# Feed-forwards: the Strassen form from the third gate/up pair on, with the sums of activations made in the first two pairs

## The chip, the cores and the metric

One NeuronCore of one Trainium2 chip runs the whole program. The metric is device time in microseconds (us) of one execution, lower is better. TensorE (PE) multiplies matrices, VectorE (DVE) and ScalarE (ACT) do elementwise work, GpSimd (POOL) does a little, and SyncE (SP) issues nearly all transfers. Each engine runs its own instructions in program order and waits for the others on semaphores.

## The reference

One layer of a streaming encoder for 640 tokens (512 of a new stream, 8 x 16 of running ones) at width 1024, in f32:

```
x += 1/2 * g1 * SwiGLU_1(mod1(RMSNorm(x)))
x += g2 * W_out [ gMLP groups || SSD heads ] (W_in mod2(RMSNorm(x)))
x += 1/2 * g3 * SwiGLU_2(mod3(RMSNorm(x)))
def swiglu(h, w1, w2):
    g, u = jnp.split(h @ w1, 2, axis=-1)
    return (jax.nn.silu(g) * u) @ w2
```

`w1` is 1024 x 5632 and `w2` is 2816 x 1024. A final modulated RMSNorm and some state outputs follow. Only the two SwiGLU feed-forwards (the first and the third line) are touched here.

## The kernel before, in words

**Precision.** Every f32 matmul is made of three reduced-precision ones: weights and activations are each split into a high part (an ACT copy into type fp32r) and a low part (DVE: value minus high part), and PE adds high x high, high x low and low x high. A weight block is therefore prepared by one ACT instruction (`blk` on ACT, L1547) and one DVE instruction (`blk` on DVE, L2122), each 128x512, before PE may read its slot. There are 7 slots (`SLOTS`) in a ring, and two buffers `raw` for the transfers (one "job" each, `load_job`).

**Feed-forward.** The hidden width 2816 is 22 tiles of 128. For each tile there is a gate/up pair `p`: the gate columns and the up columns times the 1024 rows of `hn`. Pairs come in parts of 4, 4, 4, 4, 3 and 3 (`PARTS`), and after each part its down products (eight blocks, `BLK_DOWN`) are added to `xT`.

**Two forms of a pair.** `plain_pair` multiplies 4 weight blocks (gate and up, each over two halves of the rows): 4 blocks x 4 tiles of rows x 3 products x 2 halves of the tokens = 96 matmuls of 320 columns. `wino_pair` treats the pair as a 2x2 block product (gate/up by row halves, row halves by token halves) and uses the Strassen-Winograd form with 7 products instead of 8: 7 x 4 x 3 = 84 matmuls. It needs sums of weight blocks (`first_sums` and two in `blk`: four DVE additions, L2085, in the raw buffer, `s1w`, `s2w`) and four sums of activations, T1 to T4. Pairs 0 to `PLAIN - 1` are plain, the rest Strassen. Before, `PLAIN = 3`.

**The sums of activations** are made once per feed-forward, for kk = 0 to 3. `t_sums(kk)` on DVE (L2256 to L2261) makes four 128x320 sums; `t_high(kk)` on ACT (L1686, L1687) copies the high part of T2 (320 columns) and T3, T4 (640 columns) into `tT`; `t_low(kk)` on DVE (L2267, L2269) makes the low parts. Temporaries `tst`, `xadd`, `rT` take turns over kk. T1 is handled apart: `t1_high` on ACT (L1693) and `t1_low` on DVE (L2278) overwrite a quarter of `hn_hi`, `hn_lo`, and so come after the last plain product.

**Order of the queues before.** Block numbers run through the feed-forward; plain pairs 0, 1, 2 have blocks 0 to 3, 4 to 7, 8 to 11, and Strassen pair 3 has 12 to 18. While pair `p` with first block `b` is multiplied, ACT and DVE prepare blocks `b+7` to `b+10` (or `b+13` for Strassen).

- ACT, pair 0: SiLU of gate (L1707), `t_high(0)`, blocks 7, 8, `hid_high` (L1699), blocks 9, 10. Pair 1: `t_high(1)`, SiLU, `t_high(2)`, blocks 11, 12, `hid_high`, 13, 14. Pair 2: SiLU, `t_high(3)`, 15, 16, `t1_high`, `hid_high`, 17, 18.
- DVE, pair 0: `t_sums(0)`, gate x up into `hidp` (L2303), `t_low(0)`, 7, 8, `hid_low` (L2284), 9, 10. Pair 1: `t_sums(1)`, `t_low(1)`, `t_sums(2)`, `hidp`, `t_low(2)`, 11, 12, `hid_low`, 13, 14. Pair 2: `t_sums(3)`, `t_low(3)`, 15, 16, `hidp`, `t1_low`, `hid_low`, 17, 18.

DVE reaches `t_sums(0)` only after the norm and blocks 4 to 6.

**What the first Strassen pair waits for** (`wino_pair` on PE, L1067 for the matmuls): after its first product P (bank pC), for all SiLUs of the plain pairs and for `t_ready`, that is the last `t_low`; after the second product for the snapshot of P (`snap` 1, ACT, L1730), because the third product adds onto the same bank; before the fifth for `t1_low`. ACT comes to that snapshot only when its work for the last plain pair is through.

```
product(fi, b, x, b11, True)
if p == PLAIN:
    pe.wait_ge(silu_done, fi * N_PAIR + p)
    pe.wait_ge(t_ready, 6 * fi + KQ)
product(fi, b + 1, z_bank, t3, True)
if cols is not None and p == PLAIN:
    duo_cols(cols)
pe.wait_ge(snap, 4 * n + 1)
product(fi, b + 2, x, t2, False)
```

**Between the pairs** of the first feed-forward stand small products of the conditioning vectors ("duos": `duo_rows` L966 behind pairs 1, 2, 5, 7 and so on, `duo_row` on ACT, `duo_cols` L977 on PE, `duo_sum` on DVE, L2222). In the second one they stand behind pairs 3 and 7, and two at pair 0. A transfer into `raw` waits until the low parts of the job two before are made (SP, L601, L606).

Of the kernel before, what the change touches and what calls it, by code (L numbers as in the profile page):

```python
# [25 lines left out]
FF_TILES = D_FF // P  # L26
PARTS = (4, 4, 4, 4, 3, 3)
PART0 = (0, 4, 8, 12, 16, 19)
PLAIN = 3
KQ = KD // 2  # L30
WB = KQ * P
SLOTS = 7
# [52 lines left out]
def trunk_program(nc, x_prompt, x_sample, state_ssm, state_conv, c_prompt, c_sample, w_ada, b_ada, norm_g,  # L85
# [5 lines left out]
    def sb(name, shape, dt=F32, stack=None):  # L91
        return (stack or top).enter_context(nc.sbuf_tensor(name, shape, dt))
# [13 lines left out]
    slots = [sb(f"slot{i}", [P, 2 * WB], F32R, wbuf) for i in range(4)]  # L106
# [280 lines left out]
    def t34_f(kk):  # L387
        return (xadd, rT)[kk % 2]
# [35 lines left out]
    for part, kh in enumerate(PARTS):  # L424
        for _ in range(kh):
            BLK_PAIR.append(JOB_END[-1] if JOB_END else 0)
            JOB_PAIR.append(len(JOB_END))
            JOB_END.append(BLK_PAIR[-1] + (4 if len(BLK_PAIR) <= PLAIN else SLOTS))
        BLK_DOWN.append(JOB_END[-1])
        JOB_DOWN.append(len(JOB_END))  # L430
        JOB_END += [BLK_DOWN[-1] + KQ, BLK_DOWN[-1] + KD]
    NB, JOBS = JOB_END[-1], len(JOB_END)
    SLOT0, RAW0 = (2, 4), (0, 1)
    BLOCK = {}
    for p, b in enumerate(BLK_PAIR):
        for j in range(4 if p < PLAIN else SLOTS):
            BLOCK[b + j] = ("plain" if p < PLAIN else "wino", p, j)
    for part, b in enumerate(BLK_DOWN):
# [17 lines left out]
        return n  # L456

    def slot_of(fi, b, lo, cols):
        return slots[(b + SLOT0[fi]) % SLOTS][:, lo * WB:lo * WB + cols]

    def source_of(fi, b):

# [18 lines left out]
    def wino_before(fi, p):  # L481
        return fi * (N_PAIR - PLAIN) + p - PLAIN

# [344 lines left out]
    def _(pe):  # L828
# [141 lines left out]
        def duo_cols(duo):  # L970

            pe.wait_ge(d_row, duo + 1)
            if not lane_of(duo):
                wait(pe, d_sum, duo)
            lane = lane_of(duo)
            for t in range(2):
                last = nc.tensor.transpose(q_cols[lane][:, t * P:(t + 1) * P],  # L977
                                           srow[:, lane * ADA_COLS + t * P:lane * ADA_COLS + (t + 1) * P], ident[:, :])
            last.then_inc(d_tr, 1)
# [91 lines left out]
        def wino_pair(fi, p, cols):  # L1071
# [3 lines left out]
            product(fi, b, x, b11, True)  # L1075
            if cols is not None and p > PLAIN:
# [3 lines that stand above are left out]
# [435 lines left out]
    def _(act):  # L1515
# [168 lines left out]
        def t_high(fi, kk):  # L1684
            act.wait_ge(t_sum, 3 * (KQ * fi + kk + 1))
            A(t_part(0, kk, 0, 1), t2_f(kk), ACT.Copy)  # L1686
            A(t_part(0, kk, 1, 3), t34_f(kk)[:, :], ACT.Copy).then_inc(thi_ready, 1)  # L1687
# [13 lines left out]
        def plain_pair(fi, p):  # L1701

            b = BLK_PAIR[p]
            if p == 1:
                t_high(fi, 1)
            act.wait_ge(blk_done, fi * NB + b + 2)
            A(split2(silg[:, :]), halves(acc[0]), ACT.Silu).then_inc(silu_done, 1)  # L1707
            if p == 0:
                t_high(fi, 0)
            if p == 1:  # L1710
                t_high(fi, 2)
            if p == 2:
                t_high(fi, 3)
            blk(fi, b + 7)
            blk(fi, b + 8)
            act.wait_ge(blk_done, fi * NB + b + 4)
            if p == PLAIN - 1:
                t1_high(fi)
            hid_high(fi, p)
            blk(fi, b + 9)  # L1720
            blk(fi, b + 10)
# [304 lines left out]
    def _(dve):  # L2026
# [76 lines left out]
        def blk(fi, b):  # L2103

            if b >= NB:
                return
            kind, p, j = BLOCK[b]
            w = raw[raw_of(fi, job_of(b))]
            if kind == "wino":
                n = wino_before(fi, p)  # L2110
                first_sums(fi, b)
                if j == 1:
                    if n:
                        dve.wait_ge(blk_lo, last_low[2])
                    dve.wait_ge(s_sum, 4 * n + 2)
                    s_add(s2w[:, :], s1w[:, :], w[:, 0:WB], ALU.subtract)
                if j == 3:
                    dve.wait_ge(s_sum, 4 * n + 3)
                    dve.wait_ge(blk_lo, fi * NB + b - 2)
                    s_add(w[:, 0:WB], w[:, WB:2 * WB], s2w[:, :], ALU.subtract)  # L2120
            dve.wait_ge(blk_hi, fi * NB + b + 1)
            V.tensor_tensor(out=slot_as(fi, b, 1), in0=source_of(fi, b), in1=slot_as(fi, b, 0).bitcast(F32),  # L2122
                            op=ALU.subtract).then_inc(blk_lo, 1)
            if kind == "wino":
                last_low[j] = fi * NB + b + 1
# [127 lines left out]
        def t_sums(fi, kk):  # L2253

            a, b, n = hn_f(kk), hn_f(kk + KQ), 3 * (KQ * fi + kk)
            V.tensor_tensor(out=t1_f(kk), in0=half_of(a, 1), in1=half_of(a, 0), op=ALU.subtract).then_inc(t_sum, 1)  # L2256
            V.tensor_tensor(out=half_of(t34_f(kk), 0), in0=half_of(b, 1), in1=half_of(a, 1), op=ALU.subtract)
            dve.wait_ge(t_sum, n + 1)
            V.tensor_tensor(out=t2_f(kk), in0=half_of(b, 1), in1=t1_f(kk), op=ALU.subtract).then_inc(t_sum, 1)
            dve.wait_ge(t_sum, n + 2)  # L2260
            V.tensor_tensor(out=half_of(t34_f(kk), 1), in0=half_of(b, 0), in1=t2_f(kk), op=ALU.subtract  # L2261
                            ).then_inc(t_sum, 1)

        def t_low(fi, kk):

            dve.wait_ge(thi_ready, 6 * fi + kk + 1)
            V.tensor_tensor(out=t_part(1, kk, 0, 1), in0=t2_f(kk), in1=t_part(0, kk, 0, 1).bitcast(F32),  # L2267
                            op=ALU.subtract)
            V.tensor_tensor(out=t_part(1, kk, 1, 3), in0=t34_f(kk)[:, :], in1=t_part(0, kk, 1, 3).bitcast(F32),  # L2269
                            op=ALU.subtract).then_inc(t_ready, 1)  # L2270
# [16 lines left out]
        def plain_pair(fi, p, cols):  # L2287

            b = BLK_PAIR[p]
            if p == 0:  # L2290
                t_sums(fi, 0)
            if p == 1:
                t_sums(fi, 1)
                t_low(fi, 1)
                t_sums(fi, 2)
            if p == 2:
                t_sums(fi, 3)
                t_low(fi, 3)
                blk(fi, b + 7)
                blk(fi, b + 8)  # L2300
            dve.wait_ge(blk_done, fi * NB + b + 4)
            dve.wait_ge(silu_done, fi * N_PAIR + p + 1)
            V.tensor_tensor(out=split2(hidp[:, :]), in0=split2(silg[:, :]), in1=halves(acc[1]), op=ALU.mult  # L2303
                            ).then_inc(hidp_done, 1)
            if cols is not None:
                duo_sum(cols)
            if p < PLAIN - 1:
                t_low(fi, (0, 2)[p])
                blk(fi, b + 7)
                blk(fi, b + 8)  # L2310
            else:
                t1_low(fi)
            hid_low(fi, p)
            blk(fi, b + 9)
            blk(fi, b + 10)
# [488 lines left out]
```

## Time and profile before

| what | us |
|---|---|
| median of 3 runs (lowest, highest) | 1447.94 (1447.08, 1450.46) |
| span of the profiled execution | 1443.5 |
| PE matmul busy | 1422.6 (99%) |
| DVE busy | 1014.8 (70%) |
| ACT busy | 662.9 (46%) |
| mean of all transfers | 112 GB/s |

The median is 4.4 us above the span: the span runs from the first to the last instruction, and the time has a start and an end around it. The time of the profiled execution itself is not listed, so span plus 4.4 us stands for it. A busy PE is one with a matmul in flight; the matmuls overlap, so the step from one to the next is what a matmul costs.

### The profile page before, as it was taken

How to read it: one execution, taken by the hardware profiler on the slowest of the kernel's cores; microseconds unless marked ns; L12 is line 12 of the kernel's file. 1: busy time of each engine (PE TensorE's matmuls, PEld its weight loads, DVE VectorE, ACT ScalarE, POOL GpSimd, SP SyncE). 2: the span in 40 equal slices, each digit the busy share in tenths (PEclk: the TensorE clock that was granted, in tenths of full speed). 3: DMA queues.
4: the chain of work that ended last, by engine and by line, in shares of the span. 5: the costliest groups of instructions: out<-in, count | busy, mean ns of one | idle time of the engine just before them, and what ended most of it. 6: DMA issues, size and time to landing. Idle time of an engine off the chain costs nothing.

```text
span 1443.5 us, 25671 instructions
## 1 busy us (share of the span) xinstructions
PE 1422.6 (99%) x10206; PEld 1372.1 (95%) x10206; DVE 1014.8 (70%) x1742; ACT 662.9 (46%) x1186; POOL 71.0 (5%) x121
## 2 busy tenths in 40 slices
PE   7999999999999999999999999999999999999998
PEld 6899999999999999999789999998999999999997
DVE  5667667676777776667886567557767686767776
ACT  5543525253435444576825453226425253444354
POOL 4000000000000130000100000004000000000001
PEclk9999999999999999999999999999999999999999
DMA  9752534445344612231362222444324232231221
GB/s 308 206 194 65 154 115 142 122 133 160 110 139 132 183 31 74 74 93 55 98 186 77 68 73 63 132 144 122 110 58 142 67 88 89 71 106 52 81 74 74
DMA packets 219532, 161.02 MB, mean 112 GB/s; under 512 B 6826, under 2 KB 204646, under 8 KB 219426
## 3 DMA queue, kind: packets, MB, share of 16 engines
q1 hardware_dynamic: 217026, 153.87, 35.8%
q0 software_dynamic: 1696, 5.56, 1.3%
q8 instruction: 74, 1.21, 0.4%
q14 instruction: 32, 0.26, 0.1%
q10 hardware_dynamic: 704, 0.12, 0.0%
HBM read 151.50 MB, written 8.03 MB: 111 GB/s over the span
## 4 chain that ended last, share of the span: by engine, by line
PE 92%; DVE 2%; DMA 1%; SPq 1%; ACT 1%; POOL 1%; issue 0%; DVEq 0%; ACTq 0%
PE acc L844 25%; PE acc L1176 19%; PE pC L1067 18%; PE acc L1067 14%; PE acc L1055 4%; PE pB L966 2%; PE acc L1125 2%; PE pC L1316 1%; DMA ada_raw<-in_w_ada 1%; PE pB L925 1%; DMA raw<-in_ffn_w 1%; PE pB L1301 1%; SPq L601 1%; PE pC L1451 1%; PE pC L1335 1%
## 5 line engine op out<-in xcount | busy, mean ns | idle before, releaser
L1547 ACT ACTIVATE slot<-raw 128x512 fp32r<-128x512 f32 (+1 forms) x310 | 189.5, 616 | 238.2 <-PE acc L1176 137.8
L2122 DVE TENSOR_TENSOR slot<-raw,slot 128x512 fp32r<-128x512 f32 (+1 forms) x310 | 208.4, 676 | 54.5 <-ACT slot L1547 51.9
L1176 PE MATMUL acc<-hid_hi,slot 128*128 128x320 f32 x1240 | 238.5, 310 | 0.0
L1067 PE MATMUL pC<-hn_hi,slot 128*128 128x320 f32 x912 | 216.3, 309 | 0.0
L1176 PEld LDWEIGHTS acc<-hid_hi,slot 128*128 128x128 f32 x1240 | 195.1, 188 | 2.9 <-issue 2.5
L844 PE MATMUL acc<-hn_hi,whi 128*128 128x320 f32 x672 | 161.0, 321 | 0.0
L1067 PEld LDWEIGHTS pC<-hn_hi,slot 128*128 128x128 f32 x912 | 156.2, 188 | 2.5 <-issue 2.5
L844 PE MATMUL acc<-hn_hi,wlo 128*128 128x320 f32 x672 | 153.1, 309 | 0.0
L844 PE MATMUL acc<-hn_lo,whi 128*128 128x320 f32 x672 | 153.0, 309 | 0.0
L1067 PE MATMUL acc<-tT,slot 128*128 128x320 f32 x912 | 146.3, 309 | 0.0
L1176 PE MATMUL acc<-hid_lo,slot 128*128 128x320 f32 x620 | 142.0, 308 | 0.0
L1067 PE MATMUL pC<-hn_lo,slot 128*128 128x320 f32 x456 | 140.8, 309 | 0.0
L1067 PEld LDWEIGHTS acc<-tT,slot 128*128 128x128 f32 x912 | 136.6, 188 | 0.0
L844 PEld LDWEIGHTS acc<-hn_hi,whi 128*128 128x128 f32 x672 | 111.9, 188 | 6.3 <-issue 5.9
L844 PEld LDWEIGHTS acc<-hn_lo,whi 128*128 128x128 f32 x672 | 112.3, 188 | 0.0
L844 PEld LDWEIGHTS acc<-hn_hi,wlo 128*128 128x128 f32 x672 | 112.2, 188 | 0.0
L1176 PEld LDWEIGHTS acc<-hid_lo,slot 128*128 128x128 f32 x620 | 103.8, 188 | 0.0
L2066 DVE TENSOR_TENSOR xadd<-acc,gate 128x128 f32<-128x128 f32 x95 | 27.5, 290 | 90.5 <-PE acc L1176 77.5
L2036 DVE TENSOR_TENSOR wlo<-wraw,whi 128x1024 fp32r<-128x1024 f32 x50 | 61.0, 1221 | 38.5 <-ACT whi L1529 38.0
L1067 PEld LDWEIGHTS pC<-hn_lo,slot 128*128 128x128 f32 x456 | 85.6, 188 | 0.0
L2060 DVE SCALAR_TENSOR_TENSOR xT<-acc,gate,xT 128x320 f32<-128x320 f32 (+1 forms) x190 | 82.5, 475 | 0.2 <-PE acc L861 0.2
L1067 PE MATMUL pC<-tT,slot 128*128 128x320 f32 x456 | 73.2, 309 | 0.0
(389 smaller groups left out, 2407.1 us busy)
## 6 DMA issues: line engine op xcount, KB each, us to landing
raw<-in_ffn_w SPq DMA_DIRECT2D x88, 512.0 KB, 5.2
sraw<-in_w_ada SPq DMA_DIRECT2D x26, 1024.0 KB, 7.7
wraw<-in_w_in SPq DMA_DIRECT2D x36, 512.0 KB, 3.8
raw<-in_ffn_w SPq DMA_DIRECT2D x16, 1024.0 KB, 5.1
ada_raw<-in_w_ada SPq DMA_DIRECT2D x8, 1024.0 KB, 12.0
wraw<-in_w_out SPq DMA_DIRECT2D x16, 512.0 KB, 4.1
raw<-in_ffn_w SPq DMA_DIRECT2D x8, 768.0 KB, 4.4
sraw<-in_w_ada_final SPq DMA_DIRECT2D x6, 1024.0 KB, 7.4
```

The lines of the kernel that those rows point to most:

```text
L601: sp.dma_start(kxn(w[:, 2 * d * WB:2 * (d + 1) * WB], KD, P), w1[fi][:, :, d * D_FF + p * P:d * D_FF + (p + 1) * P]).then_inc(done, 16)
L844: last = mm(acc[p][:, h * BANK:h * BANK + HALF], w[:, k, :], a[:, k * TOK + h * HALF:k * TOK + (h + 1) * HALF], start=(k == 0 and t == 0), ...
L966: last = mm(q_rows[lane_of(duo)][q * QUAD:(q + 1) * QUAD, :], c_f32[:, k, :], kxn(duo_raw(duo, j), KD, ADA_COLS)[:, k, :], start=(kk == 0) ...
L1055: last = mm(half(acc[d], h), w[:, kk * P:(kk + 1) * P], a[:, k * TOK + h * HALF:k * TOK + (h + 1) * HALF], start=(k == 0 and t == 0), stop ...
L1067: last = mm(out, w[:, kk * P:(kk + 1) * P], a, start=(first and kk == 0 and t == 0), stop=(kk == KQ - 1 and t == 2), skip_group_check=not ...
L1125: last = mm(a[h], w[t // 2][:, k, :], (hid_hi, hid_lo)[t % 2][:, k * TOK + h * HALF:k * TOK + (h + 1) * HALF], start=(k == 0 and t == 0), ...
L1176: last = mm(a[h], w[t // 2][:, k, :], (hid_hi, hid_lo)[t % 2][:, k * TOK + h * HALF:k * TOK + (h + 1) * HALF], start=(k == 0 and t == 0), ...
L1547: A(slot_as(fi, b, 0), source_of(fi, b), ACT.Copy).then_inc(blk_hi, 1)
L2036: V.tensor_tensor(out=weights(n, i, 1, w), in0=wraw[p][:, 0:w], in1=weights(n, i, 0, w).bitcast(F32), op=ALU.subtract).then_inc(wlo_done, 1)
L2060: return V.scalar_tensor_tensor(out=x[:, s:e], in0=a[s // HALF][:, p:p + e - s], scalar=gate[:, q, f * GRP:f * GRP + 1], in1=x[:, s:e], op ...
L2066: V.tensor_tensor(out=by_stream(xadd[:, SEQ:TOK]), in0=by_stream(a[1][:, SEQ - HALF:HALF]), in1=g, op=ALU.mult)
L2122: V.tensor_tensor(out=slot_as(fi, b, 1), in0=source_of(fi, b), in1=slot_as(fi, b, 0).bitcast(F32), op=ALU.subtract).then_inc(blk_lo, 1)
```

## The change

`PLAIN` becomes 2: in both feed-forwards pair 2 takes the Strassen form. Its blocks are 8 to 14, pair 3 has 15 to 21. All of the T sums move into the queues of pairs 0 and 1. The table of slots is written out so that the ring starts elsewhere in the first feed-forward; the number of blocks per feed-forward goes from 193 to 196. On PE no line is changed: the branch on `PLAIN` decides.

```diff
-PLAIN = 3
+PLAIN = 2
...
-    SLOT0, RAW0 = (2, 4), (0, 1)
+    SLOT_OF, RAW0 = ((0, 1, 2, 3, 6, 4, 5), (4, 5, 6, 0, 1, 2, 3)), (0, 1)
...
-        return slots[(b + SLOT0[fi]) % SLOTS][:, lo * WB:lo * WB + cols]
+        return slots[SLOT_OF[fi][b % SLOTS]][:, lo * WB:lo * WB + cols]
```

On ACT (`plain_pair`):

```diff
             if p == 1:
-                t_high(fi, 1)
+                t_high(fi, 2)
             act.wait_ge(blk_done, fi * NB + b + 2)
             A(split2(silg[:, :]), halves(acc[0]), ACT.Silu).then_inc(silu_done, 1)
             if p == 0:
                 t_high(fi, 0)
+                t_high(fi, 1)
             if p == 1:
-                t_high(fi, 2)
-            if p == 2:
                 t_high(fi, 3)
```

On DVE (`plain_pair`):

```diff
             if p == 0:
                 t_sums(fi, 0)
+                t_sums(fi, 1)
             if p == 1:
-                t_sums(fi, 1)
-                t_low(fi, 1)
                 t_sums(fi, 2)
-            if p == 2:
+                t_low(fi, 2)
                 t_sums(fi, 3)
                 t_low(fi, 3)
                 blk(fi, b + 7)
...
             if p < PLAIN - 1:
-                t_low(fi, (0, 2)[p])
+                t_low(fi, 0)
                 blk(fi, b + 7)
                 blk(fi, b + 8)
+                t_low(fi, 1)
             else:
                 t1_low(fi)
```

## Rows read from the trace of the kernel before

**Rows 1.** The page: busy time, and the chain that ended last, by engine.

```profile
PE 1422.6 (99%) x10206; PEld 1372.1 (95%) x10206; DVE 1014.8 (70%) x1742; ACT 662.9 (46%) x1186; POOL 71.0 (5%) x121
...
PE 92%; DVE 2%; DMA 1%; SPq 1%; ACT 1%; POOL 1%; issue 0%; DVEq 0%; ACTq 0%
```

**Rows 2.** The chain in order of time: start us, length us, what.

```profile
51.65 14.33 PE acc L1055 x96
65.97 1.86 PE pB L966 x32
67.84 14.29 PE acc L1055 x96
86.75 9.54 DMA raw<-in_ffn_w
...
130.74 1.76 PE acc L1067 x12
...
1004.69 28.39 PE acc L1055 x192
```

**Rows 3.** Waits of PE over the whole span: total us, times, longest.

```profile
PE acc L1055 <- ACT tmp L1707: 1.2, 2, 0.8
```

**Rows 4.** Timeline of DVE, second feed-forward: start, length, line, operation, idle before.

```profile
1003.34 0.48 DVE L2256 TENSOR_TENSOR hidf<-hnf 128x320 f32<-128x320 f32 x1
...
1004.66 0.49 DVE L2261 TENSOR_TENSOR xadd<-hnf,tst 128x320 f32<-128x320 f32 x1
1005.07 0.81 DVE L2303 TENSOR_TENSOR tmp<-tmp,acc 128x640 f32<-128x640 f32 x1
1006.32 0.49 DVE L2267 TENSOR_TENSOR tT<-tst,tT 128x320 fp32r<-128x320 f32 x1 [0.43 <-ACT tT L1687]
1006.73 0.82 DVE L2269 TENSOR_TENSOR tT<-xadd,tT 128x640 fp32r<-128x640 f32 x1
1007.46 1.29 DVE L2122 TENSOR_TENSOR slot<-raw,slot 128x512 fp32r<-128x512 f32 x2
1008.66 0.82 DVE L2284 TENSOR_TENSOR hid_lo<-tmp,hid_hi 128x640 fp32r<-128x640 f32 x1
1009.40 1.29 DVE L2122 TENSOR_TENSOR slot<-raw,slot 128x512 fp32r<-128x512 f32 x2
1010.60 0.19 DVE L2222 TENSOR_TENSOR modc<-pB,b_col 128x36 f32<-128x36 f32 x1
...
1011.27 0.48 DVE L2256 TENSOR_TENSOR hidf<-hnf 128x320 f32<-128x320 f32 x1
...
1014.25 0.49 DVE L2267 TENSOR_TENSOR tT<-tst,tT 128x320 fp32r<-128x320 f32 x1 [1.16 <-ACT tT L1687]
...
1019.04 0.82 DVE L2303 TENSOR_TENSOR tmp<-tmp,acc 128x640 f32<-128x640 f32 x1 [1.83 <-PE acc L1055]
...
1021.52 0.68 DVE L2085 TENSOR_TENSOR s1w<-raw 128x512 f32<-128x512 f32 x1
...
1022.84 0.69 DVE L2122 TENSOR_TENSOR slot<-raw,slot 128x512 fp32r<-128x512 f32 x1
```

**Rows 5.** Timeline of ACT there.

```profile
1013.11 0.47 ACT L1686 ACTIVATE tT<-tst 128x320 fp32r<-128x320 f32 x1 [4.11 <-DVE rT L2261]
...
1014.12 0.69 ACT L1707 ACTIVATE tmp<-acc 128x640 f32<-128x640 f32 x1
...
1034.45 0.73 ACT L1699 ACTIVATE hid_hi<-tmp 128x640 fp32r<-128x640 f32 x1
1035.08 1.14 ACT L1547 ACTIVATE slot<-raw 128x512 fp32r<-128x512 f32 x2
1036.12 0.42 ACT L1730 ACTIVATE sq<-pC 128x320 f32<-128x320 f32 x1
```

**Rows 6.** Stretches at the kernel's end: length, busy us of PE, PEld, DVE, ACT, POOL, granted clock.

```profile
1436.00:1437.00 1.00, 0.38 (x4) 0.14 (x2) 1.00 (x3) 0.00 (x0) 0.00 (x0) 1.00 1.01 373
...
1438.00:1439.00 1.00, 0.00 (x0) 0.00 (x0) 1.00 (x3) 0.00 (x0) 0.00 (x0) 0.93 1.02 379
1439.00:1440.00 1.00, 0.00 (x0) 0.00 (x0) 1.00 (x2) 0.00 (x0) 0.00 (x0) 0.50 1.02 379
```

**Rows 7.** DVE in the first feed-forward, where the first sum starts.

```profile
51.72 0.48 DVE L2256 TENSOR_TENSOR hidf<-hnf 128x320 f32<-128x320 f32 x1
```

## The prediction

> **What bounds the kernel now.** I read the page first: TensorE has a matmul in flight for 99% of the span, and the chain that ended last is TensorE for 92% [rows 1]. So a matmul removed is time gained, unless another engine then comes last. The share is an average, and the change lives in two short stretches, the first three pairs of each feed-forward. There I read the chain in order of time [rows 2], the waits of TensorE [rows 3], and the timelines of VectorE and ScalarE [rows 4, 5, 7]. What the reader is to see: the plain pairs run without a gap (96 matmuls in 14.33 us, 192 in 28.39 us), TensorE waits only 1.2 us in all for a SiLU at the edge of pair 0, and VectorE, though not the bound, cannot begin with the T sums before 1003.34 (51.72 in the first feed-forward), when pair 1 is about to start on TensorE at 1004.69 (51.65) [rows 2, 4, 7]. VectorE then has idle time, 1.83 us ahead of the gate x up product of pair 1 [rows 4], but I need to count whether that is enough.
>
> **What is saved.** A Strassen product of 12 matmuls takes 1.76 us [rows 2], so 0.1467 us a matmul. Pair 2 goes from 96 to 84 matmuls: 12 x 0.1467 = 1.76 us in each feed-forward, 3.52 us in both. The downs, the norm and the later pairs keep their matmuls, so this is the whole gain, all of it on TensorE's path.
>
> **What is moved.** Before, the last `t_low` had pairs 1 and 2 to hide behind; now the second product of pair 2 needs it, with only pair 1 and one product in front. And the blocks prepared during pairs 0 and 1 become Strassen blocks, so their weight sums come along. I add up VectorE's queue from the start of `t_sums(0)` to the end of `t_low(3)`. All steps are start to start [rows 4]:
> - one `t_sums`: 1003.34 to 1005.07, 1.73 us; four of them 6.92
> - one `t_low`: 1006.32 to 1007.46, 1.14 us; four of them 4.56
> - gate x up of pair 0 and `hid_low(0)`: the latter 1008.66 to 1009.40, 0.74 us; both are 640 columns, 1.48
> - low parts of blocks 7, 8, 9, 10: two take 1007.46 to 1008.66, 0.60 each, 2.40
> - the first two weight sums, 1021.52 to 1022.84: 1.32; the third, of the same size as a low part, 0.60. Together 1.92, newly in front of the T sums
> - in the second feed-forward alone two `duo_sum`, 1010.60 to 1011.27: 0.67
> - turns with ScalarE. For kk = 2 and 3 VectorE makes the sums, then has nothing else in its queue until ScalarE has copied the high parts: 1.16 us idle each time, as at 1014.25 [rows 4], so 2.32. ScalarE's part of it is 1.01 us, 1013.11 to 1014.12 [rows 5]. For kk = 0 and 1 other work lies between. About 0.14 us more for block 10, whose high part waits for the third weight sum.
>
> Sum: 6.92 + 4.56 + 1.48 + 2.40 + 1.92 + 2.32 + 0.14 = 19.74 us, plus 0.67 in the second feed-forward, 20.41. The last `t_low` ends at 51.72 + 19.7 = 71.5 in the first and 1003.34 + 20.4 = 1023.75 in the second; I add 0.2 us for its own tail and the hand-over: 71.65 and 1023.95.
>
> When does TensorE want it? Pair 1 is unchanged. Second feed-forward: 1004.69 + 96 x 0.1467 = 1018.77, plus P of 1.76 is 1020.53. **First stall: 3.4 us.** First feed-forward: pair 1 is followed by a duo that takes 1.86 us, so pair 2 starts where it did, 67.8, and P ends at 69.55. **First stall: 2.1 us.**
>
> **The second stall.** TensorE now does the second product, 1.76 us, to 1025.7, and wants the snapshot of P. On ScalarE this stands behind everything of pair 1, and that hangs on VectorE. After `t_low(3)` at 1023.75 VectorE makes the fourth weight sum and the low parts of blocks 11 and 12 (3 x 0.60), then gate x up of pair 1 (0.74, tail 0.1): 1026.4. Then ScalarE: `hid_high` 0.63, blocks 13 and 14 in 1.04, the snapshot 0.42 [rows 5]: 1028.5, and about 0.1 us to TensorE. 1028.6 - 1025.7 = **2.9 us.** Before, the same instructions were ready in time: the snapshot at 1036.12 ended at 1036.54, 3.6 us after the last plain matmul (1004.69 + 28.16 = 1032.85), for the two products of 3.52 us; that was a tie without slack [rows 2, 5]. In the first feed-forward the same steps start at 71.5: ScalarE is through block 14 at 75.8, `duo_row` (an estimate of 0.35 us, 256 columns beside the snapshot's 0.42 us for 320) comes before the snapshot and TensorE's `duo_cols` waits for it: 76.35 against 73.4, again 2.9 us; the snapshot is ready during `duo_cols`.
>
> Later products of pair 2 want `t1_low` (1.5 us of VectorE behind gate x up, ready about 1028.1, wanted at 1032.1), blocks 13 to 21 and the other snapshots. VectorE still has work to catch up, some 6 us, but pair 2 lasts 12.3 us and in a Strassen pair it needs about 9; I take no further stall, and let 0.5 us per feed-forward into the range. Pair 3 then finds the usual order.
>
> **Transfers.** The first down job now waits for the low part of block 14 instead of 11. That is some 8 us later (about 1029.8 by my count; before, block 11 was through at 1021.52 [rows 4]), and its first block is wanted about 10 us after that, while the slowest landing on the chain took 9.54 us behind two other transfers [rows 2]. In the first feed-forward the chain passes one transfer of 9.54 us, at 86.75, that holds the end of pair 3 by 0.4 us [rows 2]; it stands behind the duo of pair 2 in SyncE's queue, before and after alike. I cost both at nothing; the latter may give back 0.4 us.
>
> **Slots and count.** The written-out table changes which slot a block takes, not how many are in flight: nothing.
>
> **The sum.** Stalls 3.4 + 2.9 + 2.1 + 2.9 = 11.3 us, less 3.5 us saved: +7.8 us. On the span 1443.5 this gives 1451.3, and with the 4.4 us that the median has around the span 1455.7 us, 0.54% slower than 1447.94. Nothing later gives it back: everything behind waits for TensorE.
>
> Weighing a page against the rows: VectorE's 128x320 sum lasts 0.48 us, yet three of the four start 0.40 us apart, and 0.52 where one waits for the one before it: 1003.34 to 1004.66 are three steps in 1.32 us [rows 4]. The Trainium skill, VectorE: DVE Perf Modes, section "The DRAIN you can't avoid", says that the next operation waits until the pipeline is empty, and sends the reader to another section for operations that are not held. By the stricter reading each of the about 30 instructions would take its whole length, some 0.08 us more; the chain would end 2.4 us later in each feed-forward, and the time would be about 1460. The trace has 0.40, so I keep the rows.
>
> **The rivals.**
>
> *The clock falls in the stalls.* At the end of the kernel TensorE's last matmul is over at 1436.4, and the granted clock goes from 1.00 to 0.50, from 2.4 to 1.2 GHz, at about 1438.9, after some 2.5 us without a matmul [rows 6]. The new stalls are 2.1 to 3.4 us, two in a row with 1.76 us of work between. If it falls there, the products after the second stall run at half pace. Price: nothing if it comes back at once, 8.8 us per feed-forward if the remaining 60 matmuls of pair 2 all run so; I take the 2.5 us of the fall as the measure of the return: 1.25 us lost each, +2.5, 1458.2 us. For it: the row. Against it: small idle times elsewhere leave 1.00. Chance 0.33. The Trainium skill, TensorE: Matmul & The Clock Gate, section "Why this matters for your kernels", likewise warns that idle gaps between bursts of matmuls send the clock back to its lower level.
>
> *Only the T sums are late, the snapshot is not.* If VectorE and ScalarE close the distance while TensorE stands, so that the second stall falls away, it is 3.4 + 2.1 - 3.5 = +2.0: 1449.9 us, 0.14%, within 0.2%. It would need gate x up of pair 1 to be 2.9 us earlier; in the queue it is behind `t_low(3)`, so I give 0.04.
>
> *The other side: the queues keep up.* If the idle time of VectorE before (1.83 us in pair 1 and what lies in pair 2) were enough, TensorE would never stand and the 3.5 us would be whole: 1444.4 us, faster by 0.24%. The point from which it decides: the last `t_low` 3.4 us earlier and the snapshot 6.3 us earlier than I count. My count would have to be too long by a third. Chance 0.03.
>
> *More stalls than counted.* VectorE stays behind through pair 2, each product waits for its low parts or for a snapshot, and the backlog of 6 us shows for up to 3 us in each feed-forward: 1461.7. Chance 0.10.
>
> **How the numbers follow.** Forecast (two stalls in each feed-forward, clock held) 0.50, the clock 0.33, more stalls 0.10, one stall 0.04, no stall 0.03. About 0.2% (2.9 us) is what a measurement of this kernel can tell from no change. Slower by more than that: 0.50 + 0.33 + 0.10 = 0.93, of which I leave 0.01 to a time just inside the limit: 0.92. Same: 0.05. Faster: 0.03. The forecast alone spans 1453.7 to 1457.5 (1 us of error in each hand-over chain). The range for 8 in 10 leaves out the two cheap cases and the dearest part of the last: 1453.0 to 1460.5.
>
> **What the changed profile would show.** TensorE idle in front of the second product of pair 2 (L1067, `acc<-tT`), put down to VectorE's L2269, and again in front of the third, put down to ScalarE (L1730, or `srow` in the first feed-forward); VectorE without idle time in pair 1 but for the two turns of 1.16 us; SiLU of pair 1 late, at about 1018.5, and harmless; 24 matmuls fewer. I would be wrong if VectorE's queue reached `t_low(3)` before TensorE had ended P, or if the granted clock showed less than 1.00 around 1030 and 78.

## The result and the profile after

The changed kernel took 1458.7 us (median of six runs, 1455.5 to 1460.6), the kernel before 1446.8 us beside it (six runs, 1444.5 to 1450.5): 11.9 us more, ratio 1.0079, 95% interval 1.0066 to 1.0091. The forecast was 1455.7 us, with a range of 1453.0 to 1460.5. The profiled execution of the changed kernel took 1458.66 us; its span is 1457.0 us where before it was 1443.5. Time and span are 1.7 us apart here, not 4.4.

The page of the changed kernel, first the busy times, then the chain by engine; both answer to [rows 1]:

```profile
PE 1425.6 (98%) x10182; PEld 1374.3 (94%) x10182; DVE 1027.1 (70%) x1762; ACT 670.4 (46%) x1202; POOL 71.1 (5%) x121
...
PE 90%; DVE 4%; ACT 1%; POOL 1%; DMA 1%; issue 1%; SPq 0%; DVEq 0%; ACTq 0%; POOLq 0%
```

24 matmuls are gone, as the edit says, and yet TensorE is busy for 3.0 us more, and has left 2% of the chain to other engines. Both halves of the loss are in these two lines: waits, and matmuls that last longer. The waits of TensorE, total us, times, longest; the last group is the only one of them in [rows 3]:

```profile
PE acc L1067 <- issue: 5.5, 2, 3.4
...
PE pC L1067 <- ACT sq L1729: 2.6, 1, 2.6
PE pB L977 <- ACT srow L1682: 2.6, 1, 2.6
...
PE acc L1055 <- ACT tmp L1707: 1.2, 2, 0.8
```

Four stalls of 10.7 us in all. Two stand ahead of an `acc<-tT` product; "issue" there names no releaser, and VectorE's timeline has to give it. It follows here for the first feed-forward (start, length, line, operation, idle before; L2266 and L2268 are `t_low`, L2255 to L2260 `t_sums`, L2084 a weight sum, L2121 a low part, L2301 gate x up, each a line or two above its place before):

```profile
66.63 0.49 DVE L2266 TENSOR_TENSOR tT<-tst,tT 128x320 fp32r<-128x320 f32 x1 [1.16 <-ACT tT L1687]
...
70.75 0.49 DVE L2266 TENSOR_TENSOR tT<-tst,tT 128x320 fp32r<-128x320 f32 x1 [1.16 <-ACT tT L1687]
71.16 0.82 DVE L2268 TENSOR_TENSOR tT<-rT,tT 128x640 fp32r<-128x640 f32 x1
71.89 0.69 DVE L2084 TENSOR_TENSOR raw<-raw,s2w 128x512 f32<-128x512 f32 x1
...
73.70 0.81 DVE L2301 TENSOR_TENSOR tmp<-tmp,acc 128x640 f32<-128x640 f32 x1
```

The last `t_low` ends at 71.98. ScalarE's timeline behind it:

```profile
74.55 0.74 ACT L1699 ACTIVATE hid_hi<-tmp 128x640 fp32r<-128x640 f32 x1 [1.53 <-DVE tmp L2301]
75.19 1.13 ACT L1547 ACTIVATE slot<-raw 128x512 fp32r<-128x512 f32 x2
76.23 0.36 ACT L1682 ACTIVATE srow<-pB 128x256 f32<-128x256 f32 x1
76.50 0.43 ACT L1729 ACTIVATE sq<-pC 128x320 f32<-128x320 f32 x1
```

TensorE, only the lines with a stall and the products behind them, in both feed-forwards:

```profile
69.67 0.31 PE L1067 MATMUL pC<-hn_hi,slot 128*128 128x320 f32 x1
72.08 2.00 PE L1067 MATMUL acc<-tT,slot 128*128 128x320 f32 x12 [2.10 <-issue]
76.65 0.44 PE L977 MATMUL pB<-ident,srow 128*128 128x128 f32 x2 [2.56 <-ACT srow L1682]
76.97 2.98 PE L1067 MATMUL pC<-tT,slot 128*128 128x320 f32 x12
79.75 2.55 PE L1067 MATMUL acc<-tT,slot 128*128 128x320 f32 x12
82.14 0.31 PE L1067 MATMUL pC<-hn_hi,slot 128*128 128x320 f32 x1
...
1012.20 0.53 PE L1055 MATMUL acc<-hn_hi,slot 128*128 128x320 f32 x2 [0.84 <-ACT tmp L1707]
...
1031.67 1.99 PE L1067 MATMUL acc<-tT,slot 128*128 128x320 f32 x12 [3.39 <-issue]
1036.29 3.10 PE L1067 MATMUL pC<-tT,slot 128*128 128x320 f32 x12 [2.63 <-ACT sq L1729]
1039.19 2.41 PE L1067 MATMUL acc<-tT,slot 128*128 128x320 f32 x12
1041.44 0.32 PE L1067 MATMUL pC<-hn_hi,slot 128*128 128x320 f32 x1
```

The product waits until 72.08, 0.10 us after the last `t_low`; the transposes of `duo_cols` wait until 76.65, when `srow` is through. The two products behind each second stall take 5.17 us (76.97 to 82.14) and 5.15 us (1036.29 to 1041.44) instead of 3.52. Stretches of 2 us show why (length, busy us of PE, PEld, DVE, ACT, POOL, then the granted clock):

```profile
76.00:78.00 2.00, 1.35 (x8) 1.23 (x9) 2.00 (x4) 1.77 (x5) 0.00 (x0) 0.93 0.04 8
78.00:80.00 2.00, 2.00 (x9) 2.00 (x8) 1.97 (x4) 0.64 (x2) 0.00 (x0) 0.50 0.32 58
80.00:82.00 2.00, 2.00 (x12) 2.00 (x12) 1.96 (x5) 1.05 (x2) 0.00 (x0) 0.72 1.05 410
82.00:84.00 2.00, 2.00 (x16) 2.00 (x15) 1.67 (x3) 0.63 (x1) 0.00 (x0) 1.00 0.15 56
```

TensorE's clock went to its lower level, 1.2 GHz, at about 78 and came back to 2.4 GHz at about 81; 1036 to 1042 show the same (0.72, 0.50, 0.93).

**Where the time is lost.** I measure from the first matmul group behind the 0.4 us (0.8 us) wait of L1055 to the first down matmul (L1176), in the first feed-forward, and in the second from that wait to the end. The first went from 52.54 us (51.65 to 104.19) to 57.66 (51.84 to 109.50), +5.1; the second from 438.8 (1443.5 - 1004.69) to 444.8 (1457.0 - 1012.20), +6.0. That is 11.1. The stretch between went from 900.5 to 902.7, and the experiments show what of that is the change's. With 0.2 us ahead of the first mark this is the 13.5 us between the two spans; the medians are 11.9 us apart.

### The profile page after: what moved, and what is told of

Read it like the earlier page. It is cut to its first block, busy times and chain, and to the rows that moved or that the text cites. A ratio compares the mean times of both kernels' runs of the same rounds, so it can differ in the third digit from the quotient of the medians.

```text
span 1457.0 us, 25681 instructions
## 1 busy us (share of the span) xinstructions
PE 1425.6 (98%) x10182; PEld 1374.3 (94%) x10182; DVE 1027.1 (70%) x1762; ACT 670.4 (46%) x1202; POOL 71.1 (5%) x121
## 4 chain that ended last, share of the span: by engine, by line
PE 90%; DVE 4%; ACT 1%; POOL 1%; DMA 1%; issue 1%; SPq 0%; DVEq 0%; ACTq 0%; POOLq 0%
PE acc L844 24%; PE pC L1067 19%; PE acc L1176 19%; PE acc L1067 14%; PE pB L966 2%; PE acc L1125 2%; PE pC L1316 1%; PE acc L1055 1%; DMA raw<-in_ffn_w 1%; PE pB L1301 1%; PE pB L925 1%; PE pC L1451 1%; PE acc L1036 1%; PE pC L1335 1%; PE acc L861 0%
## 5 line engine op out<-in xcount | busy, mean ns | idle before, releaser
L2121 DVE TENSOR_TENSOR slot<-raw,slot 128x512 fp32r<-128x512 f32 (+1 forms) x312 | 210.4, 677 | 57.3 <-ACT slot L1547 54.5
L1176 PE MATMUL acc<-hid_hi,slot 128*128 128x320 f32 x1240 | 238.5, 310 | 0.0
L1067 PE MATMUL pC<-hn_hi,slot 128*128 128x320 f32 x960 | 227.7, 309 | 0.0
L1176 PEld LDWEIGHTS acc<-hid_hi,slot 128*128 128x128 f32 x1240 | 195.1, 188 | 2.9 <-issue 2.1
L1067 PEld LDWEIGHTS pC<-hn_hi,slot 128*128 128x128 f32 x960 | 164.4, 188 | 2.9 <-issue 2.9
L1067 PE MATMUL acc<-tT,slot 128*128 128x320 f32 x960 | 155.4, 310 | 5.5 <-issue 5.5
L1067 PEld LDWEIGHTS acc<-tT,slot 128*128 128x128 f32 x960 | 145.0, 189 | 6.0 <-issue 6.0
L1067 PE MATMUL pC<-hn_lo,slot 128*128 128x320 f32 x480 | 148.1, 309 | 0.0
L1176 PE MATMUL acc<-hid_lo,slot 128*128 128x320 f32 x620 | 142.0, 308 | 0.0
L1176 PEld LDWEIGHTS acc<-hid_lo,slot 128*128 128x128 f32 x620 | 103.8, 188 | 0.0
L1067 PEld LDWEIGHTS pC<-hn_lo,slot 128*128 128x128 f32 x480 | 90.1, 188 | 0.0
L1067 PE MATMUL pC<-tT,slot 128*128 128x320 f32 x480 | 79.1, 314 | 2.6 <-ACT sq L1729 2.6
## 6 DMA issues: line engine op xcount, KB each, us to landing
ada_raw<-in_w_ada SPq DMA_DIRECT2D x8, 1024.0 KB, 11.5
```

The lines of the kernel that those rows point to most:

```text
L1067: last = mm(out, w[:, kk * P:(kk + 1) * P], a, start=(first and kk == 0 and t == 0), stop=(kk == KQ - 1 and t == 2), skip_group_check=not ...
L1176: last = mm(a[h], w[t // 2][:, k, :], (hid_hi, hid_lo)[t % 2][:, k * TOK + h * HALF:k * TOK + (h + 1) * HALF], start=(k == 0 and t == 0), ...
```

## The experiments

The theory: VectorE's order of work makes the last `t_low` late, ScalarE's order the snapshot, and so TensorE stands twice in each feed-forward; the clock falls because it stands. Rivals: the order of the T sums costs by itself, the loss is contention or transfers, or the clock falls for a reason of its own. The first kernel is made from the one before, the others from the changed one, and all compute the same; each is compared with the kernel before on the same chip (medians 1445.9 to 1446.3).

**The order alone.** The kernel before (three plain pairs), with all four sets of T sums made within the first two.

```diff
             if p == 0:
                 t_sums(fi, 0)
+                t_sums(fi, 1)
             if p == 1:
-                t_sums(fi, 1)
-                t_low(fi, 1)
                 t_sums(fi, 2)
+                t_low(fi, 2)
+                t_sums(fi, 3)
+                t_low(fi, 3)
```

> The kernel before with only the second half of the change: PLAIN stays 3, but all four T sums and their low parts stand in the queues of pairs 0 and 1. My theory (what costs is that TensorE wants the last low part one pair earlier, not the new place of the work): pair 2 is still plain, so the queues have its 14.1 us to catch up; no stall of TensorE, time within 0.2% of before, granted clock 1.00 from 50 to 100 us and from 1000 to 1050. Rival (the crowded queues are themselves the cost): one or two stalls of 1 us or more in each feed-forward, and over 3 us slower than before.

Measured: 1446.78 against 1446.26 us, ratio 0.9999 (0.9990 to 1.0008), no stall in the third or fourth pair. The early sums cost nothing that these times show while a plain pair follows them; what costs is that a product wants them. One of the waits that are there in both kernels grew, at the end of pair 3 in the first feed-forward (1.1 us on `hid_lo`; 0.5 in a second execution of the kernel before, 0.2 in that of the changed one).

**Fillers.** The changed kernel with matmuls into an unused bank ahead of both waits, four in the first and seven in the second feed-forward ahead of the second product, five ahead of the third.

```diff
             if p == PLAIN:
+                fill((4, 7)[fi])
                 pe.wait_ge(silu_done, fi * N_PAIR + p)
...
+            if p == PLAIN:
+                fill(5)
             if cols is not None and p == PLAIN:
                 duo_cols(cols)
```

> The changed kernel with filler matmuls (ident times upto, 256 columns, about 0.47 us each, into the unused half of pC) in front of the two waits of pair 2: 4 or 7 in the first, 5 in the second, so that TensorE works while it waits; results are untouched. Theory: the waits stay (2.1, 2.6, 3.4, 2.6 us, now mostly filled), but the granted clock stays at 1.00 through pair 2, and the 3.4 us that pair 2 loses at half clock (1.7 in each feed-forward) come back: about 3.4 us faster than the changed kernel, 7 to 8 us slower than before. Rival (the clock is an accident of the run and costs nothing steady): no difference from the changed kernel beyond 1 us, 11 us slower than before.

Measured: 1453.0 us, ratio 1.0052 (1.0039 to 1.0065), 6.8 us slower than before where 7 to 8 were expected. The stretches, of this kernel and then of the changed one:

```profile
50.00:100.00 50.00, 48.84 (x358) 45.09 (x357) 39.92 (x73) 26.10 (x50) 0.00 (x0) 1.00 0.60 183
1000.00:1050.00 50.00, 48.33 (x313) 46.37 (x313) 41.89 (x74) 29.55 (x54) 2.55 (x4) 1.00 0.20 64
```

```profile
50.00:100.00 50.00, 44.96 (x329) 41.85 (x329) 39.59 (x71) 25.34 (x49) 0.00 (x0) 0.97 0.56 173
1000.00:1050.00 50.00, 43.14 (x277) 41.65 (x276) 43.15 (x75) 29.82 (x52) 6.79 (x9) 0.97 0.22 68
```

Adding matmuls makes the kernel faster. The waits end where they did, 20.22 and 24.79 us behind the mark in the first feed-forward against 20.24 and 24.81, 19.48 and 24.10 in the second against 19.47 and 24.09; what differs is the pace behind them, where the clock now holds at 1.00. The feed-forwards become 2.0 and 1.4 us shorter (55.65 and 443.4 us by the same marks), 3.4 us, as expected. The two spans are 5.8 us apart (1451.2 and 1457.0); of the rest, 2.1 us lie between the feed-forwards (900.6 against 902.7 us), which the last pair of runs takes up, and 0.3 ahead of the first.

**The snapshots alone.** The first two snapshots and `duo_row` are moved ahead of gate x up's consumers on ScalarE (ahead of `hid_high` of pair 1).

```diff
             if p == PLAIN - 1:
                 t1_high(fi)
+                first_snaps(fi)
             hid_high(fi, p)
```

> The changed kernel with the first two snapshots of pair 2 (and the duo row in the first feed-forward) moved ahead of hid_high and blocks 13 and 14 on ScalarE. Theory 1 (what TensorE waits for in the second stall is only ScalarE's order): the second stall of 2.6 us goes from both feed-forwards, 5 us faster than the changed kernel, or more if the clock then holds. Theory 2 (VectorE's backlog is behind everything, and order only moves the stall): the third snapshot stands behind block 16, whose high part waits for VectorE's weight sums of pair 3; a stall of 2.5 to 3 us appears before the fifth product of pair 2 instead, and the time is within 1 us of the changed kernel. By the sum of the queues I expect theory 2.

Measured: 1457.7 us, ratio 1.0077 (1.0065 to 1.0090): within 1 us of the changed kernel, as theory 2 has it. The second stalls are gone and stand before the fifth product instead (2.48 and 1.12 us):

```profile
PE acc L1067 <- issue: 5.5, 2, 3.4
...
PE pC L1067 <- ACT rT L1740: 3.6, 2, 2.5
```

So a wait removed is no time gained as long as the queue behind it is late: the stall follows the backlog. In the second feed-forward the product right behind the first stall of 3.40 us took 3.54 us instead of 2.00; the clock can fall after the first stall already, and the slower products shorten the stall behind them.

**The queues, without the snapshots.** Both engines' work of pairs 0 and 1 in another order: sums 0 and 1 first, then each `t_sums` a block ahead of its `t_low`, so that the turns of 1.16 us are filled.

```diff
+            t_sums(fi, 0)
+            t_sums(fi, 1)
+            gate_up(fi, 0)
+            t_low(fi, 0)
+            blk(fi, 7)
+            t_sums(fi, 2)
+            t_low(fi, 1)
+            blk(fi, 8)
+            t_sums(fi, 3)
```

> The changed kernel with the queues of pairs 0 and 1 in the new order (T sums of kk+1 in front of the low part of kk, hid_low(0) and block 10 behind the last t_low), but the first snapshots left where they were. Theory: the first stall goes (t_low(3) about 3.5 us earlier), the second stall, at the first snapshot, grows to some 3 us in the first and 4 us in the second feed-forward, since it hangs on the same VectorE queue: 7 us of stalls less 3.5 us saved, 3.5 to 4 us slower than before with the clock held, up to 7.5 if it falls. Rival (the first stall alone was the cause, and the second its echo): no stall, faster than before.

Measured: 1452.0 us, ratio 1.0046 (1.0033 to 1.0060). The first stall is gone in both feed-forwards; what is left are these two:

```profile
73.73 0.44 PE L977 MATMUL pB<-ident,srow 128*128 128x128 f32 x2 [2.25 <-ACT srow L1682]
...
1027.56 2.60 PE L1067 MATMUL pC<-tT,slot 128*128 128x320 f32 x12 [3.60 <-ACT sq L1729]
```

That is 6 us slower than before, between the 3.5 to 4 with the clock held and the 7.5 with it fallen. The clock held behind the stall of 2.25 us and fell for a moment (0.97 over 1000 to 1050) behind that of 3.60.

**Both moves together.** The new queue order and the first two snapshots early.

> The changed kernel with VectorE's and ScalarE's queues of pairs 0 and 1 written out anew: the sums for kk+1 in front of the low part of kk (no turns of 1.16 us), hid_low(0) and block 10 behind the last t_low, and the first two snapshots early. Theory (VectorE's backlog): t_low(3) is ready at about 67.7 and 1019.3 plus the shift, so the first stall is gone; the second is gone too; the backlog of VectorE is not, and one stall of about 3.7 us remains before the fifth product of pair 2, put down to the third snapshot: 4 us slower than before with the clock held, up to 7.5 if it falls. Rival (order was all that was wrong): no stall, 3.5 us faster than before.

Measured: 1454.65 us, ratio 1.0062 (1.0049 to 1.0074). One stall in each feed-forward, as expected, at the third snapshot: 3.60 us at 78.68 and 3.68 us at 1034.10, and the clock at 0.97 in both stretches. At 8.4 us slower than before it is beyond the 7.5 that the theory allowed; 0.9 us of the profiled execution is a wait for `gm_bias`, which the last pair of runs takes up. The median is above that of the queue order alone (1454.65 against 1452.0), though the two intervals overlap. The traces say where: the first feed-forward takes 56.3 us by the marks used above, against 53.7, and the second 442.2 in both. The third snapshot stands behind block 16, which waits for VectorE's weight sums, so the single stall of the first feed-forward is 3.60 us instead of 2.25, and the clock falls behind it.

**All four snapshots first.** As in the kernel with both moves, and in pair 2 every snapshot goes ahead of block 16 on ScalarE, every sum of the C parts ahead of the low parts on VectorE.

```diff
+            if p == PLAIN:
+                snapshot("s1", x, 3)
+                snapshot("s2", x, 5)
+                for j in range(8, 13):
+                    blk(fi, b + j)
```

> As e5_both, and in pair 2 all four snapshots on ScalarE in front of block 16, and the three sums of products on VectorE in front of the weight blocks 17 to 20. Theory (what is left is VectorE's amount of work, not its order): the stalls of 3.7 us shrink to 0.7 and 1.0 us at the third snapshot, and a stall of 1.2 to 1.4 us comes up behind it (pair 3, or the duo behind pair 2); 4 to 4.5 us of stalls against 3.5 us saved: within 0.2% of before, clock 1.00. Rival (order was all): no stall and 3.5 us faster than before.

Measured: 1445.5 against 1445.9 us, ratio 1.0000 (0.9991 to 1.0009), 12 us less than the changed kernel, each against its own runs of the kernel before, with the same instructions in another order. The stalls on TensorE:

```profile
76.05 0.41 PE L1067 MATMUL pC<-hn_hi,slot 128*128 128x320 f32 x1 [0.53 <-ACT rT L1729]
86.27 0.44 PE L977 MATMUL pB<-ident,srow 128*128 128x128 f32 x2 [0.84 <-ACT srow L1682]
...
1028.74 0.41 PE L1067 MATMUL pC<-hn_hi,slot 128*128 128x320 f32 x1 [0.60 <-ACT rT L1729]
1038.67 2.02 PE L1067 MATMUL pC<-tT,slot 128*128 128x320 f32 x12 [0.87 <-ACT sq L1729]
```

The clock holds in both feed-forwards. Four short stalls, 2.84 us idle and 3.5 us counted from start to start, use up what the 24 matmuls give: the feed-forwards take 52.3 and 438.8 us, against 52.5 and 438.8 before.

**A third engine.** The kernel above with the T sums of tiles 2 and 3 made on GpSimd.

> As e6_early, and the T sums of kk = 2 and 3 made on GpSimd, which is idle there, right after the norm, into spare parts of hidf; VectorE has 3.46 us less to do in each feed-forward. Theory (amount of VectorE's work): if GpSimd makes its eight 128x320 sums within about 15 us, no stall is left in pairs 2 and 3, the gain of 3.5 us shows whole, 1442.7 us, 0.24% faster than before. Rival (sharing: the trace before has GpSimd's 128x128 operation at 0.40 us alone and at 0.93 to 0.98 us beside a busy VectorE, and VectorE's 640-column product at 1.02 us there): the sums take over 2 us each, GpSimd is late with kk = 3 or VectorE slows down, stalls of 2 us and more in a feed-forward, no gain over e6_early.

Measured: 1451.5 us, ratio 1.0038 (1.0025 to 1.0052), 6 us slower than without GpSimd. VectorE's groups by form, with GpSimd at work (first) and in the kernel above without it (second), 50 to 62 us; columns: busy us, mean ns of one:

```profile
L719 DVE TENSOR_TENSOR hidf<-hnf 128x320 f32<-128x320 f32 x2 | 2.3, 1162 | 0.0
L720 DVE TENSOR_TENSOR xadd<-hnf 128x320 f32<-128x320 f32 x1 | 1.2, 1158 | 0.0
...
L724 DVE TENSOR_TENSOR rT<-hnf,tst 128x320 f32<-128x320 f32 x1 | 0.5, 491 | 0.0
```

```profile
L2306 DVE TENSOR_TENSOR hidf<-hnf 128x320 f32<-128x320 f32 x3 | 1.4, 483 | 0.0
L2307 DVE TENSOR_TENSOR xadd<-hnf 128x320 f32<-128x320 f32 x2 | 1.0, 484 | 0.0
```

The same sum takes 1.16 us instead of 0.48 while GpSimd makes its own of 1.00 to 1.38 us, and 0.49 again once GpSimd is through (59.3 us). Nothing is gained by making them side by side: VectorE reaches gate x up of pair 0 at 60.50 instead of 55.41. The rival was right in this, though the sums did not take its 2 us. TensorE gets a new stall for it, ahead of pair 1's up half, on gate x up of pair 0: 2.55 us in the first feed-forward and 1.14 in the second. Behind the one of 2.55 us the clock fell, and the matmuls of 320 columns start 0.27 us apart instead of 0.15:

```profile
62.00:64.00 2.00, 2.00 (x10) 2.00 (x9) 2.00 (x4) 2.00 (x5) 0.00 (x0) 0.50 0.00 0
```

The Trainium skill, SBUF — State Buffer, section "SBUF: two separate sides", says that a VectorE operation with two SBUF inputs and a GpSimd operation that reads SBUF shut each other out for the whole instruction; the trace agrees.

**Less backlog still.** The kernel of the four early snapshots, with T sums 0 and 1 of the first feed-forward moved into VectorE's idle time in the norm before it, and two `duo_sum` of the second moved behind pair 2.

```diff
                 first_scale(j // 2)
+                if j > 2:
+                    t_sums(0, j // 2 - 2)
                 low(j, FIRST_TILE[j])
```

> The version with all four snapshots early, and two moves more. In the first feed-forward the sums of activations of the first two tile pairs are made in VectorE's idle time between the norm's last low parts (stretches of 1.9 us idle there, a set of four sums takes 1.73 us); in the second the two sums for the modulation vectors (0.67 us) are made after the third gate/up pair instead of within the second. Theory (what idles TensorE in the third pair is the backlog of VectorE and ScalarE and nothing else, so work taken out of it comes back as time): the idle of 0.53 and 0.84 us in the first feed-forward goes, and in the second 0.60 goes with some 0.9 left. 2.0 us less than the version before it: 1443.5, ratio to before about 0.9985. Rival (the remaining idle is the turn of one snapshot or one sum behind its product, whatever the queues hold): both feed-forwards keep 0.5 and 0.9, 1445.5, ratio 1.000. Second rival (the early sums delay the norm's low parts, and so the first pair's products): the first pair starts up to 1 us later, 1446.5.

Measured: 1447.0 against 1446.1 us, ratio 1.0006 (0.9997 to 1.0015). The stalls of the first feed-forward are what they were:

```profile
75.94 0.42 PE L1067 MATMUL pC<-hn_hi,slot 128*128 128x320 f32 x1 [0.53 <-ACT rT L1729]
86.15 0.44 PE L977 MATMUL pB<-ident,srow 128*128 128x128 f32 x2 [0.84 <-ACT srow L1682]
```

The idle is 0.53 and 0.84 us as before, though VectorE had reached gate x up of pair 0 at 51.83 instead of 55.41. So work taken out of VectorE's queue did not come back as time, and the first rival has the lengths right. Its reason, the turn of one snapshot whatever the queues hold, is not what the trace shows. The time freed on VectorE went into a wait of its own. Three lines of the two timelines, in order of time, say why:

```profile
69.94 0.44 ACT L1758 ACTIVATE sq<-pC 128x320 f32<-128x320 f32 x1 [2.46 <-PE pC L1067]
...
71.20 0.69 DVE L2170 TENSOR_TENSOR slot<-raw,slot 128x512 fp32r<-128x512 f32 x1 [4.38 <-ACT slot L1547]
...
73.27 0.74 ACT L1699 ACTIVATE hid_hi<-tmp 128x640 fp32r<-128x640 f32 x1 [1.13 <-DVE tmp L2433]
```

ScalarE has nothing to do for 2.46 us until TensorE ends P, because the first snapshot stands ahead of blocks 11 and 12 in its queue. VectorE waits 4.38 us for the high part of block 11 (1.38 in the kernel without the two moves). Then come the low parts of blocks 11 and 12, gate x up, `hid_high`, three blocks, and at 75.48 the third snapshot, which TensorE waits for. This chain starts at TensorE's own product, so an earlier VectorE cannot shorten it; with VectorE busy without a gap from 71.20 to 85.05, the wait for `srow` hangs on the same start. Blocks 11 and 12 ahead of the first snapshot, with the later snapshots early, was not tried. No order tried beats the kernel before.

**The two kernels once more**, for a second profiled execution each.

> The changed kernel once more, for a second profiled execution. Theory of the stalls: they are in the order of the queues, so they come again at the same places with the same lengths within 0.1 us (2.1 and 2.6 in the first feed-forward, 3.4 and 2.6 in the second), and the clock falls behind them again. The 2.2 us that the changed kernel's execution lost between the feed-forwards are put down to a fall of the clock at 624 to 628 us that comes and goes between executions: if so, this one may show the distance to before at 12 or at 13.5 us, by whether the clock falls there. If the loss is a consequence of the change's order of work, it comes again with the clock held.

> The kernel before once more, for a second profiled execution: no idle stretch over 1.2 us in the third gate/up pair, and the clock at 1.00 from 60 to 600 us. At 610 to 640 us, where the changed kernel's clock fell, it may fall here too, which would show that this loss isn't the change's; the span is then 1445 instead of 1443.5.

Measured: 1459.1 and 1447.1 us, spans 1457.4 and 1445.5. The stalls came again: 2.1, 2.6 and 3.4 us, but the fourth took 1.1 instead of 2.6, for this time the clock fell within the third, and the product between them took 3.54 us. The changed kernel, in the second feed-forward:

```profile
1028.00:1030.00 2.00, 0.31 (x3) 0.04 (x1) 1.17 (x3) 0.76 (x2) 0.00 (x0) 1.00 0.00 0
1030.00:1032.00 2.00, 0.31 (x1) 0.34 (x2) 1.63 (x3) 2.00 (x5) 0.00 (x0) 0.60 0.00 0
1032.00:1034.00 2.00, 2.00 (x9) 2.00 (x9) 2.00 (x4) 0.63 (x2) 0.00 (x0) 0.50 0.00 0
```

And the kernel before, in the middle of the kernel:

```profile
616.00:620.00 4.00, 4.00 (x34) 3.87 (x33) 1.86 (x3) 1.23 (x3) 0.81 (x2) 0.98 0.21 45
620.00:624.00 4.00, 4.00 (x18) 3.91 (x18) 3.95 (x5) 3.59 (x10) 0.00 (x0) 0.60 0.98 258
624.00:628.00 4.00, 4.00 (x30) 3.52 (x29) 1.18 (x2) 3.67 (x4) 0.00 (x0) 1.00 0.00 0
```

The clock falls at this place in the kernel before too, though not in its first profile, and without a stall of TensorE. Its stretch between the feed-forwards is 902.0 us then instead of 900.5, so 1.5 of the 2.2 us in the first comparison were not the change's. The rest, 0.5 to 0.7 us, is one wait, `PE pB L1443 <- DMA gm_bias<-in_gm_b`: 0.7 and 0.5 us in the two executions of the changed kernel, none in the three executions of kernels with three plain pairs. It is 0.5 to 0.9 us in the other kernels with two plain pairs as well, 0.7 in the one that is as fast as before, and absent only in the one with the fillers. Why that transfer lands later was not settled.

## Why the prediction was right, and where it was not

The likeliest case had the clock held and gave 1455.7; what came is the rival with the clock fallen, named at 1458.2, and 1458.7 was measured. That these two are 0.5 us apart is partly luck. The 4.4 us put on top of the span are not a start and an end: time and span are 1.5 to 1.8 us apart in every execution that lists both (1458.66 and 1457.0, 1447.13 and 1445.5). The other 2.8 us came in because the profiled execution of the kernel before, 1445.1 us by its span, was faster than the median beside it. As differences, the forecast was +7.8 us, the rival +10.3, and +11.9 was measured.

- **The saving** (1.76 us each): 24 matmuls less, right.
- **First stalls** (2.1 and 3.4 us): 2.10 and 3.39, and for the reason given. The chain of 19.74 us to the last `t_low` ended at 71.98 for 71.5 and both turns of 1.16 us are there. TensorE ended P at 69.82 for 69.55, of which 0.2 us is the later start of the pair. The four sums from 67.78 to 69.10 start 0.40, 0.40 and 0.52 us apart, as the span of the four in [rows 4] has it, so their durations of 0.48 us don't add up whole, and the 1460 us of the stricter reading did not come.
- **Second stalls** (2.9 us each): 2.56 and 2.63 as idle time. The forecast counted from start to start. So counted, the first stalls are 2.26 (69.67 + 0.147 to 72.08) and 3.55 us, the second 2.81 (72.08 + 1.76 to 76.65) and 2.86: 11.5 us, where 11.3 was forecast. A stall costs the idle time and 0.15 to 0.25 us more, in which the last matmul ends alone. Two slips in the working changed nothing: 1036.54 is 3.7 and not 3.6 us after 1032.85, and 75.8 with 0.35 and 0.1 is 76.25, not 76.35.
- **The clock**: the step that failed is the clock held through the stalls, chance 0.50, against "the clock falls in the stalls", 0.33. It fell in both feed-forwards in both profiled executions of the changed kernel. Its price was put at 1.25 us each, read off the time it took to fall at the kernel's end [rows 6]; the first execution shows 1.65 and 1.63 us (5.17 and 5.15 less 3.52). The kernel with the fillers shows it by itself: the same waits, the clock held, 3.4 us less. The sum by measured terms: 11.5 + 3.3 - 3.5 = 11.3 us, where the two feed-forwards show 11.1 (11.6 in the second execution).
- **Against the fall** I had only that small idle times leave 1.00. The row for it was the better evidence: 2.5 us without a matmul were enough at the end of the kernel, and 3.4 us is longer than that. A fall of the clock behind two stalls with one product between them should have been the likelier case.
- **No further stall in pair 2** (0.10 for more): none was seen, but not because the queues had caught up. With the earlier waits gone the next snapshot is late by 2.5 to 3.7 us; the first two stalls gave ScalarE and VectorE the time for it. This was a hit by the number and not by the reason, "pair 2 lasts 12.3 us and in a Strassen pair it needs about 9".
- **Transfers at nothing**: right in the feed-forwards. The wait for `gm_bias`, 0.5 to 0.7 us, was not seen coming.
- **The queues keep up** (0.03): in the order given they don't. In another order they nearly do, and the kernel is then even with the one before, not faster.

## What to carry over

When work is moved ahead of its consumer, add up each in-order queue from its first free moment to the last instruction wanted, start to start, and compare with the consumer's own clock; that gave four stalls within 0.2 us, start to start. Then ask of each stall whether TensorE stands as long as it does somewhere else in the trace where the clock falls, and price the products behind it at the lower level. And do not mend the first wait alone: write out the whole queue behind it, since the next one shows up as soon as the first is gone. The order in each queue was worth 12 us here, with the same work.

## What was not expected of the hardware

- The granted clock fell after 3.4 us without a matmul in one execution at once (0.60 over 1030 to 1032), and in another only behind a product of 2.0 us and a second stall of 2.63 us. The same kernel, the same stall of 3.39 us: so its length alone doesn't decide. A single stall of 2.25 us left the clock up, and one of 2.55 us, in the kernel with GpSimd, brought it down. The Trainium skill, TensorE: Matmul & The Clock Gate, section "Why this matters for your kernels", likewise warns of idle gaps between bursts; these runs show that it differs from one execution to the next.
- It also fell with TensorE busy without a gap, at 620 to 624 us in the kernel before, soon after sixteen matmuls of 8 columns and into ones of 320: these start 0.27 us apart there instead of 0.15, and 1.5 us are lost. It comes and goes between executions of one kernel.
- Nine filler matmuls of 256 columns in one feed-forward and twelve in the other (each of them two in the trace) held the clock and left the waits as long as they were: 3.4 us gained with nothing computed.
- GpSimd's 128x320 sums made VectorE's beside them 2.4 times as long, 0.48 to 1.16 us, so that eight sums moved off VectorE freed none of its time.
